# Dealing the last head's output matmuls over nine steps, and moving two query rotations ahead of the output norm

## The reference, cut to what matters

```
# first block, one layer
o = rms_norm(gla_out, norm_g) * silu(gate)                 # GLA output norm and gate
q, k = rope_2d(rms_norm(q, qn_g)), rope_2d(rms_norm(k, kn_g))
o = softmax(q k^T / 8) v                                   # 8 query heads on 2 key heads
xs = xs + gate_x * ((sigmoid(p13)*ya + sigmoid(p14)*yb + sigmoid(p15)*yc) @ w_out)

# second block, one layer
for each head and each chunk c, in order:                  # state R carried from chunk to chunk
    s = (q_c k_c^T) * Dmat
    o_c = s v_c + xi * (q_c R);   R = g * R + (k_c * zeta)^T v_c
y_r = head_layernorm(ret, gn_r) * silu(rz)
x = x + gate * (concat([y_m, y_r]) @ w_out)                # 2048 -> 1024
```

## Time and profile before

| | |
|---|---|
| median of 3 runs | 3299.59 us (3297.2 to 3299.6) |
| the profiled execution | 3300.26 us, span 3298.3 us |
| granted TensorE clock, mean | 0.978 |
| busy share of the span | PE 96%, PEld 70%, DVE 41%, ACT 26%, POOL 47% |
| chain that ended last | PE 86%, DVE 8%, POOL 2%, ACT 2%, issue 1% |

### The profile page before, as it was taken

One profiled execution on the slowest core, in us unless ns is written; L12 is line 12 of the kernel. 1 busy time (PEld: TensorE's weight loads), 2 busy tenths in 40 slices (PEclk: granted clock), 3 DMA queues, 4 the chain that ended last, 5 costly groups with the idle time before them and its releaser, 6 DMA issues.

```text
span 3298.3 us, 40515 instructions
## 1 busy us (share of the span) xinstructions
PE 3164.9 (96%) x15123; PEld 2302.9 (70%) x15123; DVE 1366.0 (41%) x2573; ACT 846.0 (26%) x1547; POOL 1539.9 (47%) x1451
## 2 busy tenths in 40 slices
PE   7999998999999999998989999999998999999989
PEld 4666675665656555465778768888994688889955
DVE  3021346544564412226666555444332363443322
ACT  4122226421111022324411222332111123322111
POOL 1688987000000059971353325776550157775600
PEclk9999999999999999998999999999999999999999
DMA  6111110023443121110233422222221222222202
GB/s 222 52 39 32 31 35 14 14 79 125 128 138 130 41 64 39 45 39 1 68 115 116 140 66 77 72 70 77 65 77 51 66 77 77 65 77 65 76 28 75
DMA packets 259907, 236.59 MB, mean 72 GB/s; under 512 B 20950, under 2 KB 257410, under 8 KB 259716
## 3 DMA queue, kind: packets, MB, share of 16 engines
q1 hardware_dynamic: 259716, 234.02, 23.4%
HBM read 231.91 MB, written 2.10 MB: 71 GB/s over the span
## 4 chain that ended last, share of the span: by engine, by line
PE 86%; DVE 8%; POOL 2%; ACT 2%; issue 1%; SPq 1%; DMA 0%; DVEq 0%; ACTq 0%; POOLq 0%
PE ps L481 27%; PE ps L1219 23%; PE ps L526 11%; PE ps L1053 5%; PE ps L512 3%; DVE arena L1905 2%; PE ps L1277 2%; PE ps L796 2%; DVE arena L1909 1%; PE ps L1321 1%; PE ps L809 1%; ACT arena L1375 1%; PE ps L1158 1%; DVE bQz L1909 1%; DVE small L2176 1%
## 5 line engine op out<-in xcount | busy, mean ns | idle before, releaser
L2604 POOL TENSOR_TENSOR arena<-arena,posi 128x512 f32<-128x512 f32 (+1 forms) x360 | 412.3, 1145 | 30.0
L481 PE MATMUL ps<-hT,wring 128*128 128x512 f32 (+1 forms) x1184 | 406.4, 503 | 0.7 <-ACT arena L1375 0.7
L526 PE MATMUL ps<-hT,wring 128*128 128x512 f32 (+1 forms) x1024 | 376.9, 523 | 0.4 <-ACT arena L1375 0.2
L481 PEld LDWEIGHTS ps<-hT,wring 128*128 128x128 f32 x1184 | 228.3, 194 | 170.1 <-issue 155.5
L1375 ACT ACTIVATE arena<-ps 128x256 f32<-128x256 f32 (+4 forms) x395 | 171.6, 434 | 642.4 <-PE ps L481 235.2
L2686 POOL TENSOR_TENSOR arena<-wring 128x512 f32<-128x512 f32 x72 | 91.8, 1275 | 491.8 <-PE ps L1219 297.2
L526 PEld LDWEIGHTS ps<-hT,wring 128*128 128x128 f32 x1024 | 194.1, 194 | 154.0 <-issue 145.1
L481 PE MATMUL ps<-arena,wring 128*128 128x512 f32 (+1 forms) x768 | 278.7, 523 | 3.0 <-issue 3.0
L2603 POOL TENSOR_SCALAR posi<-arena,cols 128x512 f32<-128x512 f32 (+1 forms) x360 | 245.7, 683 | 35.4
L1905 DVE TENSOR_TENSOR arena<-arena 128x768 f32<-128x768 f32 (+7 forms) x120 | 171.2, 1426 | 192.8 <-ACT arena L1375 188.9
L1375 ACT ACTIVATE arena<-ps,cols 128x512 f32<-128x512 f32 (+2 forms) x172 | 100.8, 586 | 545.8 <-PE ps L481 298.6
(11 more groups left out here) (271 smaller groups left out, 5068.1 us busy)
## 6 DMA issues: line engine op xcount, KB each, us to landing
wring<-in_w_in SPq DMA_DIRECT2D x126, 1024.0 KB, 5.4
wring<-in_w_mod SPq DMA_DIRECT2D x24, 1024.0 KB, 8.6
wring<-in_w_out SPq DMA_DIRECT2D x24, 1024.0 KB, 5.8
wring<-in_w_ada SPq DMA_DIRECT2D x21, 1024.0 KB, 5.2
wring<-in_w_conv_out SPq DMA_DIRECT2D x7, 512.0 KB, 6.1
wring<-in_w_gla_out SPq DMA_DIRECT2D x7, 512.0 KB, 6.1
wring<-in_w_attn_out SPq DMA_DIRECT2D x7, 512.0 KB, 5.5
arena<-in_w_ada SPq DMA_DIRECT2D x3, 1024.0 KB, 5.2
```

The source lines that it names most:

```text
L481: last = eng.matmul(o_(out), a, b_, start=(i == 0), stop=(i == len(parts) - 1))
L526: mm = eng.matmul(bank[b][:, 0:n], w[:, k, j * P:(j + 1) * P], hT[:, k, t0:t0 + n], start=(k == 0), stop=(k == KD - 1))
L2604: pool.link(eng.tensor_tensor(dst, dst, scratch, ALU.add))
```

## The change

1. In the last head of both layers of the second block, the 42 early output matmuls (3 output tiles of 14) are no longer placed as three runs of 14 behind the first three parts of the core. `OUT_SHARES` deals them as 3, 5, 4, 5, 4, 6, 4, 7, 4 behind its nine parts, in the same order. The wait for head 6's output moves from the first of them to the 13th; the first waits for head 5's alone. Banks 6 and 5 are claimed where their first matmul now stands.
2. In out2 the `claim(4, 5)` is taken out.
3. In both layers of the first block the rotations of query tiles 2 and 3 stand before the spread of the second GLA norm, on TensorE and on VectorE, and the reciprocal of the query norms stands before them on VectorE.
4. In the second layer GpSimd waits for VectorE's GLA scaling before its four half sums.

```diff
+OUT_SHARES = [3, 5, 4, 5, 4, 6, 4, 7, 4]
...
         if n == HEADS2 * 2:
-            a = [[("out", n, j)] for j in range(OUT_EARLY)]
+            ends = np.cumsum(OUT_SHARES).tolist()
+            a = [[("out", n, e - share, e)] for e, share in zip(ends, OUT_SHARES)]
...
                 turned("q", 1)
-                next(between, None)
-                gla_spread(l, 1)
                 turned("q", 2)
                 next(between, None)
                 turned("q", 3)
+                next(between, None)
+                gla_spread(l, 1)
...
                     if kind == "out":
-                        j = x[0]
-                        if j == 0:
-                            rings[0] = LAST_HEAD
-                        claim(7 - j)
-                        w_out.append(weights(wv(I["w_out_2"][l], j * P, P), 16, P))
-                        out_plan.append(len(plan) - 1)
-                        eng.wait_ge(*at(("ys", l, 6)))
-                        for k in range(14):
+                        rings[0] = LAST_HEAD
+                        for j, k in (divmod(i, 14) for i in range(*x)):
+                            if k == 0:
+                                claim(7 - j)
+                                w_out.append(weights(wv(I["w_out_2"][l], j * P, P), 16, P))
+                                out_plan.append(len(plan) - 1)
+                            if j == 0 and k in (0, 12):
+                                eng.wait_ge(*at(("ys", l, 6 if k else 5)))
                             eng.matmul(bank[7 - j][:, 0:TX], w_out[j][:, k, :], ys[:, k, :], start=(k == 0), stop=False)
...
                     plan[out_plan[j]][1] = ("full", key)
-                claim(4, 5)
                 rings[0] = {"A": [0, 1], "V": [2, 6, 3, 1]}
...
                 rotated("q", 1)
-                gla_scaled(l, 1)
-                m.mark(("branch", l, 1), *m.at[("gla out done", l, 1)])
-                rotated("q", 2)
-                rotated("q", 3)
                 u0 = units(l)[0]
                 eng.wait_ge(*at(("free", ("qss", l))))
                 rcp(qscale[:, :, u0:6, :], qscale[:, :, u0:6, :], ("q inverse", l))
+                rotated("q", 2)
+                rotated("q", 3)
+                gla_scaled(l, 1)
+                m.mark(("branch", l, 1), *m.at[("gla out done", l, 1)])
                 attend(l)
...
             eng.wait_ge(*at(("full", ("ag", 1, 3, "x"))))
+            eng.wait_ge(*at(("gla out done", 1, 1)))
             four_sums(quarter, h_sums1, ("h sums1",))
```

## The result

The changed kernel takes 3263.07 us (median of 4 runs, 3259.88 to 3266.1) beside 3298.39 us of the kernel before (4 runs, 3294.52 to 3299.6): ratio 0.9895, 95% interval 0.9878 to 0.9912. That is 35.3 us faster. The profiled run took 3264.25 us with a span of 3262.5 us.

The account below looks back on a forecast made before the run. TensorE, busy 96% of the span, was taken as the bound. Last heads 24.0 us plus attention 3.2 gave 27.2 us off 3300.26: 3273.1 us, as a median 3272.4; range 3267 to 3280.

Parts of the forecast that it names:

- How the numbers follow: Closing step for the whole kernel: forecast keeps 0.53, 8-in-10 range 3267 to 3280 us, faster with chance 0.96.
- the bounds of the claim: In out2 of the second block's last heads: removing the claim gains between 0 and 1.5 us per layer.
- The last heads: Second block, both layers: waits, claim and clock give 13.8 us in the first, 10.2 in the second, 24.0 together.
- The claim: At line 481 in out2: the 1.48 us wait is the claim of bank 5; removing it gains 1.5 us per layer.
- The clock: Second block's last heads: with waits gone full clock returns, giving 4.6 and 1.8 us; bounds 0 and 6.4.
- the rival in which it does not come back: Last heads: waits go but the clock stays low, 6.4 us stay: 3278.8 us. Chance 0.12.
- the slower rival: Last heads: lower clock takes the whole last head, up to 53 us more per layer: 3378 us. Chance 0.02.
- The attention: First block's second layer: third pair's scores come 3.2 us earlier, each small product ending with a half sum; bounds 0, 8.0.
- The rival that nothing is blocked: Attention's start: half sums do not hold up VectorE, gain 8.0 us instead of 3.2: 3267.6 us. Chance 0.12.
- The rival that the half sums eat the whole gain: Attention's start: products and copy blocked longer, only the last heads gain: 3275.6 us. Chance 0.15.
- Thin shares: Last heads: filler too short for some chain per chunk, half their gain lost: 3287.6 us. Chance 0.06.

Follow-up runs that it names:

- after: Profiled run of the changed kernel, all four parts, against the kernel before: 3264.25 us, span 3262.5 us.
- whole: The changed kernel run again with nothing edited, first repeat: 3269.77 us, ratio 0.9907 to the kernel before.
- banks: Changed kernel with early output tiles 0 and 1 in banks 6 and 7 instead of 7 and 6 in the second block's second layer: 3267.08 us, single run.
- heads: Kernel before plus parts 1 and 2 only (output matmuls dealt out, no claim in out2): 3273.59 us, ratio 0.9919.
- thin: Changed kernel with shares 9, 9, 9, 1, 4, 1, 4, 1, 4, leaving one output matmul before later turns: 3283.27 us, ratio 0.9946.
- attention: Kernel before plus parts 3 and 4 only (rotations ahead of the norms, half sums behind the scaling): 3300.01 us, ratio 0.9995.
- poolwait: Kernel before plus part 4 only (GpSimd waits for VectorE's GLA scaling before the half sums): 3308.09 us, single run.
- shares: Kernel before plus part 1 only, matmuls dealt out but claim(4, 5) kept in out2: 3273.26 us, ratio 0.992.
- fine: Changed kernel with the four half sums at the attention's start cut into eight instructions of half the length: 3264.5 us, ratio 0.9899.
- rotations: Kernel before plus part 3 without part 4 (no GpSimd wait; last heads unedited): 3299.25 us, single run.
- late_banks: Changed kernel with the half sums moved to the attention's end and early output tiles of the second layer in other banks: 3271.96 us, ratio 0.9918.
- again: The changed kernel run once more with nothing edited, second repeat: 3268.61 us, ratio 0.9911 to the kernel before.

## Why the prediction was right or wrong

**The range.** 3267 to 3280 held the medians of both repeats, 3269.77 and 3268.61, and not the 3263.07 of the result. The step that failed is "How the numbers follow": its range took in the rivals and the bounds of the claim and had no term for the clock in code that is not touched. A single profiled run carries it on both sides. Of the 35.8 us between the two spans 27.2 were forecast, 3.0 are terms that were mis-sized, as below, and 5.6 came in stages without an edit. The mean clock of the profiled runs rose by 0.005, the change itself explains 0.0031, and the 0.0019 left are 4.8 us at 2.5 us per 0.001. The same stages vary between kernels that are alike there: from the second layer's first product to its GLA norm +2.4 (after), 0.0 (whole), -3.6 (banks), and from the first layer's next tile to the second layer's first early output matmul from -6.4 (heads) to +0.1 (thin). That the repeats gave 27.1 and 29.1 us, so near to the 27.2 of the forecast, is in part luck too: all 16 runs gave 32.4 in the mean, and the touched places 30.2 in the trace.

**The last heads, 24.0 us forecast, 26.6 measured: mis-sized.** The mechanism is the one forecast, wait by wait. Short was the price of a wait. I took the idle time in brackets. In the earlier trace rows's stretch before, the timeline of TensorE reads:

```profile
3196.79 0.38 PE L1305 MATMUL ps<-const,arena 128*128 128x128 f32 x2
3198.83 0.44 PE L1326 MATMUL ps<-const,arena 128*128 128x128 f32 x2 [1.67 <-DVE arena L1907]
3199.16 0.70 PE L1313 MATMUL ps<-arena 128*128 128x256 f32 x2
```

From line 1305's start to the instruction behind the turn it is 2.37 us; covered, in after, it is 0.44 (2475.93 to 2476.37). The wait costs 1.93 where its bracket says 1.67: 0.26 us more. thin says the same from the other side, 4.25 us for brackets of 3.60, or 0.22 more for each of three; the claim cost 0.16 more (1.64 for 1.48), and so did the wait that banks takes away (1.57 for 1.41). Five such waits a layer (three turns, the join, the next tile) are 0.8 to 1.3 us, most of the 1.2 and 1.4 us that each layer gave above the forecast (15.0 for 13.8, 11.6 for 10.2). The 11.6 us themselves are those of one trace of before: in attention and poolwait, whose last heads are as before, the second layer's took 1.4 and 1.3 us longer.

**The claim, 1.5 us forecast per layer:** 1.64 and 1.65 by shares. Right.

**The clock, 4.6 and 1.8 us:** the windows give 5.0 and 1.8 at the lower level before and none after. Right, and the rival in which it does not come back fell. So did the slower rival: the clock is 1.00 over both last heads. In thin it did not fall either, though bare turns returned.

**The attention, 3.2 us forecast, 3.6 measured in the trace.** Each product did end with a half sum, the first transposes came 5.5 us earlier relative to the first scores (14.16 us after them before, 8.68 in after), and the third pair waits for the copy (2.67 us). The 0.4 us above the forecast are the chain of the half sums: I had set the four products 2.57 us apart (1518.3 to 1526.0), and they end 2.42 apart (1510.30 to 1517.57), a half sum and the opening behind it. The clock, from which I counted no gain, rose from 0.63 to 0.78 in the mean and made TensorE's work 0.7 us shorter (6.21 in place of 6.95), but TensorE waits for VectorE's copy there, so this gave the third pair nothing. The first row is of before, the second of after:

```profile
1512.70:1529.99 17.29, 6.95 (x28) 4.06 (x29) 14.84 (x18) 5.75 (x9) 10.26 (x6) 0.63 0.00 1
```
```profile
1504.15:1518.31 14.16, 6.21 (x29) 3.79 (x29) 13.68 (x15) 6.64 (x11) 10.05 (x5) 0.78 0.00 1
```

The rival that nothing is blocked fell with the products of 1.39 to 1.50 us, and fine, rotations and late_banks move the blocking with the half sums. The Trainium skill states in "SBUF — State Buffer", section "Who interferes with whom", that an instruction of VectorE with two SBUF inputs contends with one of GpSimd that reads SBUF; these traces agree, 1.50 us for an instruction of 0.16. The rival that the half sums eat the whole gain fell in the trace; the medians alone could not have told.

**Thin shares:** no wait before a turn was left, so that rival fell. Its 3287.6 us were summed wrongly: they leave out the 3.2 us of the attention, with which they are 3284.4. The kernel thin shows what too thin shares cost: 8.5 us in the trace, and a median of 3283.27 us.

What stays open: why the granted clock in unchanged code differs between runs, and so how wide the range should have been, and whether the 3.6 us of the attention are all in the device time.

## What to carry to other kernels

Filler is worth what stands right in front of the instruction that would wait: five to seven matmuls ahead of each turn took away all 6.9 us of waits that the same 42 matmuls in three blocks left in each layer. Price a wait that goes at its bracket plus the restart (0.16 to 0.26 us here), and add what the lower clock took in the work around it. When you move an engine's work out of one blocked chain, look which two-input instruction it meets next, and cut it short instead of moving it (here 3.1 us more in the trace, though the medians do not tell it apart). Give every forecast from one profile a margin for the granted clock, and compare timed runs at equal clock before you believe 5 us.

## What the runs showed of the hardware

The mean granted clock of one and the same kernel lay between 0.975 and 0.984 over 50 runs, and the span followed it, 3310.5 to 3283.8 us, while the dealt last heads repeated to 0.01 us from trace to trace (46.76 us in the first layer, in after, whole, again, heads, fine and banks). With the bare turns the second layer's took 55.03 us before and 56.41 in attention. Between two half sums of GpSimd there is an opening of 0.07 to 0.08 us (after: one ends at 1510.28, the next begins at 1510.36), and VectorE's product of 0.16 us ends in it: the product is begun, held, and let go when the other engine's instruction ends. Cutting GpSimd's instruction from 2.35 to 1.26 us made the four products 0.31 to 0.42 us long. Both engines can pay: beside VectorE's sums of two SBUF tensors GpSimd's half sum took 2.67 and 2.68 us, beside the small products 2.34 to 2.36.
